# A hybrid layer on one Trainium2 core: three blocks of 2, 3 and 3 token tiles instead of four blocks of two

## What is computed

```python
proj = h @ w_in                      # 6160 columns: q/k/v/z/a/b, FoX q/k/v/f, two gates
y_a = _gdn_branch(...)               # conv + SiLU, L2 norm, chunked delta rule, gated norm
y_b = _fox_branch(...)               # causal attention with cumulative forget gates, 8 heads of 64
mix = sigmoid(gate_a) * y_a + sigmoid(gate_b) * y_b
h = layernorm(alpha * h + mix @ w_o)
# _peer: 8 heads, top 16 of 128 on two sides, top 16 of their sums -> 128 experts of 16384 a token
act = gelu(einsum('td,tkd->tk', h, u_tab[expert])) * gate
y = einsum('tk,tkd->td', act, v_tab[expert])
h = layernorm(alpha * h + y)
```

## Time and profile before

| | us |
|---|---|
| three timed runs | 3583.01, 3581.53, 3570.33 |
| their median | 3581.53 |
| profiled execution, first to last instruction (span) | 3575.8 |
| PE busy in it | 2446.3 (68%) |
| DVE busy | 2097.0 (59%) |
| POOL busy | 2209.1 (62%) |
| ACT busy | 655.0 (18%) |
| bytes moved | 1290.18 MB, mean 361 GB/s |
| of them by the gathers' queue | 1073.87 MB |

### The profile page before, as it was taken

The page is one execution under the profiler, slowest core; times in us unless marked ns, Lnnn a source line. Parts: engine busy times, 40 slices in busy tenths (PEclk is TensorE's granted clock), DMA queues, the critical chain, the costliest instruction groups (busy, mean ns, idle before and its releaser), DMA issues.

```text
span 3575.8 us, 37418 instructions
## 1 busy us (share of the span) xinstructions
PE 2446.3 (68%) x12224; PEld 1513.4 (42%) x12224; DVE 2097.0 (59%) x4939; ACT 655.0 (18%) x1652; POOL 2209.1 (62%) x2093
## 2 busy tenths in 40 slices
PE   8889993677976876667977877766797730133354
PEld 6676872444754544434735544433564310000000
DVE  5134899875477675554358776554447669744400
ACT  3331322332022213321003212321101000000000
POOL 1000577677547765677556766677767667777774
PEclk9899996888998987777988988867898865566588
DMA  5323999899989999999999999999999999999998
GB/s 171 91 87 136 363 401 360 336 392 402 409 312 373 400 412 360 350 381 384 415 402 351 408 405 394 369 377 371 398 413 410 409 410 409 410 409 409 409 410 324
DMA packets 367626, 1290.18 MB, mean 361 GB/s; under 512 B 39596, under 2 KB 68148, under 8 KB 362308
## 3 DMA queue, kind: packets, MB, share of 16 engines
q0 software_dynamic: 294912, 1073.87, 76.8%
q1 hardware_dynamic: 66760, 201.33, 15.2%
q10 hardware_dynamic: 5760, 12.59, 0.9%
HBM read 1274.65 MB, written 12.98 MB: 360 GB/s over the span
## 4 chain that ended last, share of the span: by engine, by line
PE 24%; DMA 22%; POOL 17%; DVE 16%; issue 15%; ACT 3%; DVEq 3%; ACTq 0%; POOLq 0%; SPq 0%
DMA ring<-in_ev,idxT 12%; PE banks L1570 10%; POOL ring L818 8%; DVE ring L1260 8%; POOL ring L804 8%; DMA ring<-in_eu,eidx 5%; PE banks L1580 4%; PE banks L1559 4%; DMA arena<-in_eu,eidx 3%; PE banks L1855 2%; PE banks L1702 1%; PE banks L1621 1%; DMA wslot<-in_w_mix 1%; POOL arena L818 1%; POOL arena L804 1%
## 5 line engine op out<-in xcount | busy, mean ns | idle before, releaser
L804 POOL DMA_INDIRECT ring<-in_eu,eidx x938 | 1044.4, 1113 | 875.5 <-DVE eidx L1529 393.4
L818 POOL DMA_INDIRECT ring<-in_ev,idxT x894 | 950.9, 1064 | 380.0 <-issue 245.7
L1559 PE MATMUL banks<-ring,wide 128*32 128x512 f32 x3576 | 631.5, 790 | 530.5 <-DMA ring<-in_ev,idxT 460.5
L1260 DVE CUSTOM_DVE_ANT_0 ring<-ring,h_cur 128x1024 f32<-128x1024 f32 x663 | 782.6, 1221 | 192.1 <-DMA ring<-in_eu,eidx 190.1
L1570 PE MATMUL banks<-arena,wslot 128*128 128x256 f32 (+2 forms) x3280 | 747.2, 386 | 21.9 <-DMA wslot<-in_w_pq 12.5
L1570 PEld LDWEIGHTS banks<-arena,wslot 128*128 128x128 f32 (+1 forms) x3280 | 622.4, 194 | 179.2 <-issue 70.9
L1559 PEld LDWEIGHTS banks<-ring,wide 128*32 128x32 f32 x3576 | 120.1, 130 | 851.7 <-DMA ring<-in_ev,idxT 431.5
L1260 DVE CUSTOM_DVE_ANT_0 ring<-ring,banks 128x1024 f32<-128x1024 f32 x275 | 329.3, 1217 | 110.8 <-DMA ring<-in_eu,eidx 106.8
L1580 PE MATMUL banks<-arena 128*128 128x128 f32 x1408 | 216.2, 312 | 42.3 <-ACT arena L995 26.1
L1580 PEld LDWEIGHTS banks<-arena 128*128 128x128 f32 x1408 | 202.9, 223 | 79.7 <-ACT arena L995 33.5
L1559 PE MATMUL banks<-arena,wide 128*32 128x512 f32 x520 | 138.6, 868 | 118.6 <-DMA ring<-in_ev,idxT 64.5
(11 more groups left out here) (302 smaller groups left out, 2810.9 us busy)
## 6 DMA issues: line engine op xcount, KB each, us to landing
wslot<-in_w_pq SPq DMA_DIRECT2D x64, 576.0 KB, 8.3
wslot<-in_w_mix SPq DMA_DIRECT2D x24, 1536.0 KB, 9.8
wslot<-in_w_qkv SPq DMA_DIRECT2D x48, 512.0 KB, 7.0
wslot<-in_w_fqk SPq DMA_DIRECT2D x32, 512.0 KB, 7.6
ring<-in_eu,eidx POOLq DMA_INDIRECT x938, 12.6
wslot<-in_w_out SPq DMA_DIRECT2D x7, 2048.0 KB, 10.4
ring<-in_ev,idxT POOLq DMA_INDIRECT x894, 12.4
wslot<-in_w_z SPq DMA_DIRECT2D x16, 512.0 KB, 6.7
```

What stands on the lines that cost most here:

```text
L804: pool.indirect_dma_start(out=place(UPOS[k]), out_offset=None, in_=eu, in_offset=bass.IndirectOffsetOnAxis(ap=eidx[:, n % (2 * TT), c // T ...
L818: pool.indirect_dma_start(out=place(VPOS[k]), out_offset=None, in_=ev, in_offset=bass.IndirectOffsetOnAxis(ap=idxT[:, n % (2 * TT), t:t + ...
L1260: dve.tensor_tensor_reduce(out=row, in0=row, in1=hp[0] if held else h_cur[:, n % 3, :] if n < NT - TT else hp[n % 2], scale=1.0, scalar=0. ...
L1559: last = pe.matmul(BY[k][32 * j:32 * j + 32, :], wide32[:, at:at + 32], place(VPOS[4 * q + j])[:, k * 512:(k + 1) * 512], start=(m == 0), ...
```

## The change

`TILES = [2, 3, 3]` takes the place of `T` and `TT`: block 0 is as before, blocks 1 and 2 have 384 tokens, and there is no fourth block. With it come:

- The arena grows to 18464 floats, the ring shrinks to 15 places, `NX` grows to 11, and the semaphores of the gathers in flight go from 16 and 8 quads to 12 and 6.
- For blocks 1 and 2 the scaled queries are stored to DRAM (`d_fq`) by ACT's queue and loaded into `qa` by SP; ACT copied them before. z is stored to `d_z` and loaded a tile at a time into `zch`.
- SP issues the gate rows of a block's first tile in `nrm` (in `rT` before) and loads `x` in the first `wo` (in `ot` before), after the last `mix`.
- Queries and scores of a head use the same two banks `B[0]` and `B[1]`, 384 columns each; PE waits for the scores of the head before to be out (`s_sce`). The one-hot step of `sel` goes over the two sides in turn.
- DVE's `nrm` waits for the stores of FoX q, k and v.
- In `pace()`: `SECOND` 192, and the plan for the dots of earlier blocks runs half way into the last choice (`WHEN`). `SHARE` is the same for all widths.
- In block 0 the second half of `w_out` lands in eight pieces.

```diff
-NR = 18
-NX = 9
-NU, NQ = 16, 8
+STEPS = [FH * n for n in TILES]
+BEFORE_STEPS = [sum(STEPS[:b]) for b in range(NB)]
+ARENA = 18464
+NR = 15
+NX = 11
+NU, NQ = 12, 6
...
-SECOND, VSECOND = 160, 64
+SECOND, VSECOND = 192, 96
+WHEN = 0.5
...
-    total = sum(share(kind, b) for kind, b, i in UNITS[first + 1:alone])
+    until = alone + round(WHEN * (last - alone))
+    total = sum(share(kind, b) for kind, b, i in UNITS[first + 1:until])
...
-            ready, lately = T * b + TOPK * i, 0
+            ready, lately = START[b] + TOPK * i, 0
...
-                want = SECOND + round((T * (NB - 1) - SECOND) * (run - levels) / (total - levels))
+                want = SECOND + round((START[NB - 1] - SECOND) * (run - levels) / (total - levels))
...
+            def nrm(b, i):
+                if b:
+                    sp.wait_ge(s_rowst, 16 * (b + 1))
+                    sp.wait_ge(s_scr, PH * b + 1)
+                    gates(FROM[b])
+                    sp.wait_ge(s_ixT, transposed(FROM[b - 1]))
+                    sp.wait_ge(s_zst, 48 * b)
+                    chunk_of_z(b, 0)
...
+            def queries_of(b, i, j):
+                sp.dma_start(qa[b][0:FD, j, :], d_fq[i, FD * j:FD * (j + 1), START[b]:START[b + 1]]).then_inc(s_qa[j], 16)
...
                 if mm == 0 and 0 < i < FH // 2 - 1:
-                    sp.wait_ge(s_O, MA * b + m)
+                    sp.wait_ge(s_O, BEFORE_STEPS[b] + m)
                     head(b, i + 1)
+                if b and m < STEPS[b] and ((mm == 0 and i) or (mm == TILES[b] and i + 1 < FH // 2)):
+                    for r in range(2):
+                        sp.wait_ge(s_S[r], BEFORE_STEPS[b] // 2 + (m + 1 - r) // 2)
+                    queries_of(b, i if mm == 0 else i + 1, 1 if mm == 0 else 0)
...
             def wo(b, i):
+                if b and i == 0:
+                    for j in range(2):
+                        sp.wait_ge(s_mix[j], 4 * (b + 1))
+                    tokens(b)
...
+                    if b:
+                        act.wait_ge(s_fev[0], 4 * b + i + 1)
+                        act.dma_start(d_fq[i, :, START[b]:START[b + 1]], fqst[:, i % 2, :]).then_inc(s_fqst[i % 2], 16)
...
+                    dve.wait_ge(s_fvst, 16 * FROM[b + 1])
+                    for j in range(2):
+                        dve.wait_ge(s_fqst[j], 16 * 2 * b)
+                        dve.wait_ge(s_fkst[j], 16 * 2 * (b + 1))
...
             def queries(b, i):
                 pe.wait_ge(s_pqe, PH * b + i + 1)
+                if b:
+                    pe.wait_ge(s_sce, PH * b + i + 1)
                 for j in range(2):
                     arrived(b, "pq", 2 * i + j)
-                    last = block_mm(B[0][:, j * T:(j + 1) * T], item("pq", 2 * i + j, 9), h1T)
+                    bank = B[j][:, 0:WIDTH[b]] if b else B[0][:, j * WIDTH[0]:(j + 1) * WIDTH[0]]
+                    last = block_mm(bank, item("pq", 2 * i + j, 9), h1T[b])
```

More of the change, by code:

```diff
@@ L14 @@
 KB = D // P
-T = 256
-NB = SEQ // T
-TT = T // P
 NT = SEQ // P
+TILES = [2, 3, 3]
+NB = len(TILES)
+FROM = [sum(TILES[:b]) for b in range(NB + 1)]
+WIDTH = [P * n for n in TILES]
+START = [P * n for n in FROM]
+BLOCK = [b for b in range(NB) for _ in range(TILES[b])]
+HOLD = 5
 GH = 4
@@ L86, in order @@
             units += [("idx", 0, 1)] if b == 1 else []
-            units += [(kind, b, i) for kind, i in ATTEND[:1] + DELTA[-1:] + ATTEND[1:] + MERGE]
+            units += [(kind, b, i) for kind, i in steps[:1] + chain[-1:] + steps[1:] + merge(TILES[b])]
         after = PROJECT if b + 1 < NB else []
@@ L106, in summed_at @@
 def summed_at(b, i):
-    return 2 * TT * b + ([j for kind, j in FIRST if kind == "wo"].index(i) if b == 0 else i) + 1
+    return 2 * FROM[b] + ([j for kind, j in FIRST if kind == "wo"].index(i) if b == 0 else i) + 1
 def share(kind, b):
@@ L142, in pace @@
         else:
-            run += share(kind, b) if n < alone else 0.0
+            run += share(kind, b) if n < until else 0.0
             if n < second:
@@ L396, in build, with at, each @@
-        st, mv = r.take(TT, 2, 6), r.take(2)
+        def at(start, *shape, rows=P):
+            n = 1
+            for d in shape:
+                n *= d
+            assert start + n <= ARENA, (start, n)
+            v = arena[0:rows, start:start + n]
+            names = ("a", "b", "c")[:len(shape)]
+            if len(shape) > 1:
+                v = v.rearrange("p (" + " ".join(names) + ") -> p " + " ".join(names), **dict(zip(names[:-1], shape[:-1])))
+            return v
+        def each(make):
+            return [make(b, WIDTH[b], TILES[b]) for b in range(NB)]
@@ new lines, in scores @@
+            def scores(b, i):
+                act.wait_ge(s_scr, PH * b + i + 2)
+                act.wait_ge(s_top, PH * b + i)
+                if b == 0:
+                    both = B[1][:, :].rearrange("p (a b c) -> p a b c", a=2, b=TILES[0])
+                    act.activation(kept[:, i, :, :], both[:, :, 1, :], ACT.Copy)
+                    act.activation(sc[0][:, :, 0, :], both[:, :, 0, :], ACT.Copy).then_inc(s_sce, 1)
+                    return
+                for j in range(2):
+                    last = act.activation(flat(sc[b][:, j, :, :]), B[j][:, 0:WIDTH[b]], ACT.Copy)
+                last.then_inc(s_sce, 1)
@@ L1132, in first_head @@
                                ACT.Copy).then_inc(s_pqe, 1)
                 act.wait_ge(s_scr, tt + 1)
[L1134 removed]
+                act.activation(kept[:, 0, :, :] if tt else sc[0][:, :, 0, :], both[:, :, tt, :], ACT.Copy).then_inc(s_sce, 1)
             def fst(b, i):
@@ L1289, in sv @@
                 dve.drain()
-                dve.tensor_tensor(L, L, rows, ALU.add)
+                dve.tensor_tensor(L, L, line, ALU.add)
                 dve.tensor_scalar(A, V, 0.0, None, ALU.max)
```

767 lines of the change are left out of this document (396 added, 371 removed).

## The result

| | before, us | changed, us |
|---|---|---|
| median of the timed runs | 3581.7 | 3786.7 (3781.73 to 3793.85) |
| ratio | | 1.0593, 95% interval 1.0571 to 1.0615 |
| profiled execution (span) | 3575.8 | 3780.0 |

The changed kernel is 5.9% slower, 204 us of span. The forecast was 3652 with a range to 3740: the sign was right, the size about a third of what came (+70 of +205).

A forecast was written before the change was run, and what follows sets the result against it. Nearly every stage was taken as filled with gathers until two limits meet, among PE, DVE, POOL and DMA. Priced stage by stage, the terms summed to 3646 us of span; with 5.7 added the forecast was 3652, range 3535 to 3740.

The forecast's parts named there:

- E: Second choice with the projection of block 2: 384 us, from 359.5 us of PE at a share of 0.936.
- the hole: About 200 us with no gather issued, between the attention and the first `sel` of block 1.
- the tail: Last stage, almost only gathers: 792 of them where it held 516, 276 more at 1.288 us, 1031 us in all.
- F: Delta rule of block 2: 210 gathers at 1.40 us each, 294 us.
- G: Attention of block 2: 184 gathers of 1.47 us each, 271 us.
- B: Delta rule of block 1: 260 us, with DVE at 256 and 190 gathers at 245 to 279.
- Rival 3: The ring of 15 starves: a gather takes 1.76 us in E, F and G, 177 us more, 3829; chance 0.10.
- I: Last choice: 250 us, from 220 us of DVE at a share of 0.881.
- C: Attention of block 1: 139 us, from 88 gathers of 1.47 us and 10 us of waits for query loads.
- A: First choice with the projection of block 1: 275 us, from 257.9 us of PE at a share of 0.936.
- D: Merge of block 1, with no gather: 188 us, from 176.5 us of PE at a share of 0.936.
- rival 2: PE loses its gaps in the first two choices and both merges: 67 us less, 3585 us; chance 0.17.

The follow-up runs named there:

- a_plan: Changed kernel with second-choice dots spread, block 0's last dots spread into the merge, query loads ahead of keys, SECOND 160 and VSECOND 64; 3668.43 us, ratio 1.0270.
- a_spread: Changed kernel with at most 2 dots planned behind a unit, not 8, from block 1's first selection to the end of its choice; 3731.24 us, ratio 1.0446.
- a_small: Changed kernel with every gather cut to 512 bytes a row, dots and v matmuls still over 1024 columns; 3688.21 us.
- a_fill: Changed kernel with the last 64 dots of block 0 spread up to block 1's first `sel`, not kept within the attention; 3762.61 us, ratio 1.0519.
- b_hole: Kernel before with no gather planned in block 1's merge, its 71 row sets spread over later units; 3623.34 us, ratio 1.0124.

## Why the prediction was right and wrong

**Right.** The sign, and in part the reason: with another plan (a_plan) the kernel is still 2.7% slower, up to the first `sel` longer by 161 us and behind it shorter by only 72. The split at the end of E was forecast as 239 later and 169 back; it came as 349 later (1701 for 1352) and 145 back. The bytes, the hole, the tail (1031 against 1033) and a gather's price in F (304/219 = 1.39 for 1.40) and G (1.47, 250/170) are near or at their terms; G had 170 records where 184 were taken. For the tail there is some luck in it: POOL's issue, at 1.24 us, would have held it to nearly the same time as the transfer at 1.288. And a_plan's 3668 lies near the 3652, but with gains in it (the hole filled, stage B relieved) that the sum did not have.

**Wrong: stage E, +85.** The failed step is "359.5 at 0.936": PE's share was carried over from the merge, a stage whose gathers lie evenly, to one whose plan I had in the table only at its ends (256 at `top`, 368 at `nrm`). I counted 216 row sets as 1.74 us each, a mean, and did not look at how they lie between one `sel` and the next. PE's work came out close (351 us for 359.5), but its share was 0.75, not 0.936. The row of this very stage before has 258.45 of 349, 0.74; at that share the term would have been 485. There the DMA engines were at a share of 0.97, and I took the stage for one at two limits, near each other, that could be priced one by one; in the changed kernel the engines wait for one another with no limit reached (DMA at 0.87 after the first head). a_spread shows that the order of the row sets is 65 us of it, while an eighth of the bytes brought only 26 (a_small, 443). Which of a_spread's 404 us are the 20 over the forecast is open: its last 23 us, from the index table to `nrm`, with PE busy for 4, are the plainest gap. The first head is not: PE is busy for 53.6 of its 58 us, though no gather starts in its first 40, as its own `sel` is the first to give row sets. The v columns of the sum should also have been 104 by its table, not 100, which is 3 us.

**Rival 3, the ring, was dismissed too quickly.** It was set aside by "in attention POOL's own work, not a place, is on the chain". The price of a place, 11 in the kernel before, is 33 us for three over the whole, not 177; F and G took 1.39 and 1.47 us a gather, not 1.76, and E, at 2.1 (469/222), hardly changed with 13 places, so the mechanism by hold time is not what the runs showed. Two more places taken cost time in F, G, H and I (63 us together), which the sum had at nothing.

**B, +36, and I, +23.** In B the share 0.881 of DVE did not carry over: DVE is busy for 224.5 us, as forecast (226), but of 296. POOL waited there 28 us for dots and 26 for PE in the longest waits of the stage, and a row set took 1.57 us; the bound of 1.47 was too low. a_plan, with 64 row sets fewer due in B and some 62 us less of it, shows that the row sets due there, with their dots, were the limit to price. In I, DVE was busy for 204 where 220 was forecast, and of 273; no run takes that stage by itself.

**C, +18.** 10 were taken for the query load, 18.5 came, at the two places named. The rest is 10 us, with 78 records for the 88 gathers, a gather's price: with 46 of them the attention took 109 (a_fill).

**A and D, -16 each.** PE's work was forecast as 257.9 and 176.5, and measured as 252.2 and 166.8; the share of 0.936 was wrong in the other direction: 0.97 in both, at a granted clock of 1.00, the 2.4 GHz level. About half of the 32 us is the smaller work, half the share. The share is as rival 2 had it; that weight loads made the gaps before is not shown, but gathers did not: b_hole's narrow merge, with 23 of them in place of 67, has PE busy for 125.9 of 142 us. The Trainium skill, "TensorE: Matmul & The Clock Gate", "Step-by-step", has the next weights load during the present matmul; these two stages agree, with 160 us of weight loads beside 252 of matmuls in 259, and 93 beside 167 in 172. In E the gaps were waits.

## What to carry to other kernels

A stage's mean price for a transfer holds only if the transfers lie evenly; look at what the plan has due between its release points, and how long ahead of that each transfer can start. Work that is made per larger block moves between the parts of a kernel: it is added where it is last and taken away where something else is last, and the two don't cancel. A buffer place had a price that climbed as places went (11 us, then 21), so a change that takes three of them has to be charged for them, even where the waits for places look small.

## What the runs showed of the hardware

A gather with 512 bytes a row is not cheaper for POOL than one with 4096: 1.12 and 1.05 us against 1.08 and 1.03 a record, and in the tail a median of 0.94 with 0.30 between in both kernels. With an eighth of the bytes the tail of 792 gathers took 1036 us, where it was 1033.
